# A recurrent mixer with fp32 gate and block products, and the last output panel of the split products summed in one half of its PSUM bank

## The chip, the cores and the metric

The kernel runs on one core of one Trainium2 chip. Its time is the device time of one execution in microseconds: 3352.14 us is the median of three runs (3350.11 to 3352.18). The engines are PE (TensorE, matmul), DVE (VectorE), ACT (ScalarE), POOL (GpSimd) and SP, which here issues the loads of the weights.

## The reference, cut to what matters

A residual stream x of 256 tokens and 1024 features goes through six layers. Each is a feed-forward sublayer, a mixer, and a second feed-forward sublayer, so there are 12 feed-forward sublayers (FFN) and 6 mixers: HGRN, differential attention, pooling, HGRN, a hybrid of a state-space model and attention (HYB), and the recurrent mixer (REC). Each sublayer normalizes its input and its output:

```python
h = swiglu_2(rms_norm(x, g[0]), ffn_w_in, ffn_w_out)      # silu(x @ gate) * (x @ up) @ w_out, d_ff = 2816
x = x + 0.5 * rms_norm(h, g[1])
h = recurrent_mixer(rms_norm(x, g[2]), ...)
x = x + rms_norm(h, g[3])

def recurrent_mixer(h, w_in, conv_w, conv_b, w_a, b_a, w_x, b_x, lam, w_out):
    gate, xr = jnp.split(h @ w_in, 2, axis=-1)            # 1024 -> 2 x 1024
    gate = jax.nn.gelu(gate, approximate=True)
    xr = causal_conv(xr, conv_w, conv_b)                  # 4 taps along the tokens
    return (rg_lru(xr, w_a, b_a, w_x, b_x, lam) * gate) @ w_out

def rg_lru(x, w_a, b_a, w_x, b_x, lam):                   # 8 blocks of 128 x 128 in w_a and in w_x
    r = sigmoid(block_product(x, w_a) + b_a)
    i = sigmoid(block_product(x, w_x) + b_x)
    log_a = 8 * r * log_sigmoid(lam)
    a = exp(log_a)
    u = sqrt(-expm1(2 * log_a)) * (i * x)
    return scan of s[t] = a[t] * s[t-1] + u[t]
```

## The kernel before

**Layout.** Everything lies by feature: h and the like are [128 partitions, 8 feature tiles, 256 tokens]. Weights come in panels of 1 MB (128 x 2048 fp32) that SP loads into 5 slots (raw); panel g is asked for when panel g - 5 is done.

**Split products.** Most products are made of fp32r parts. ACT copies a panel to whi (1.9 us), DVE makes wlo = raw - whi (2.3 us), which together is called a split. The input is split too: xs (or hs in the second half of an FFN) holds hi in columns 0:256 and lo in 256:512. `tile_product` (L1886, L1887) then does whi x [hi | lo], 512 columns, and wlo x hi, 256 columns, into a PSUM bank of 512 columns. The result is the sum of the bank's two halves. So ACT first copies the right half to corr (L1572) and DVE adds it to the left one (L1744), into tsum or y.

**Whole products.** The output projections of the mixers other than HYB read raw as plain fp32 with 256 moving columns (L2010). Each such product is two records in the trace, its result needs one half of the bank and no corr, and its panel no split. These panels are called whole.

**FFN.** 22 panels in, 11 out. Of the 11, seven ("wide") hold two rows of weights for all eight output tiles, and four hold the last eight rows for one pair of output tiles each. Both kinds add to the same banks. HYB's projection is built so with four wide panels.

**The close of a sublayer.** ACT squares the output tiles, PE sums the squares over the partitions (L1997, L2002, L2004, L2006, each two records), ACT makes the reciprocal root (L1504, L1506), DVE updates h (L1723, L1725) and splits it for the next sublayer, whose first two panels open with L1909 and L1911. The last two tiles, 6 and 7, are handled by themselves in `close_sublayer`: where the last panel is split, each goes corr (ACT, L1563), y (DVE, L1717), square (ACT, L1566); where it is whole, ACT squares the bank. Ten small matmuls (L1988) stand before the next sublayer's first product.

**REC.** PE does six split panels (four of x, two of the gate), the block products of W_a and W_x as split products in four quarters (L366, L367), two more gate panels, and the whole output projection. Between readouts DVE does the convolution with all its taps (L378, L385) pair by pair and splits its result for the block (L223). Then come sigmoids (ACT, L265), log a, i x conv, Exp and Tanh (ACT, L270, L275), one minus a squared (DVE, L333, L336), its root (ACT, L280), the products and scans (DVE, L345, L347), Gelu (ACT, L282) and the gated product (DVE, L351), which the projection waits for.

**What sets the order.** Each engine's instructions stand in the order in which its function (`act_rec`, `dve_rec`, `pe_rec`; `read_out` calls a hook after each panel) writes them, and it waits on named semaphores. Nothing reorders them.

Of the kernel before, what the change touches and what calls it, by code (L numbers as in the profile page):

```python
# [9 lines left out]
F32 = mybir.dt.float32  # L10
F32R = mybir.dt.float32r
# [47 lines left out]
def build(nc, a, out):  # L59
# [22 lines left out]
    for l in range(2):  # L82
# [13 lines left out]
    log1ps = hgrns = seconds = 0  # L96
    for n, s in enumerate(subs):
        s["n"], s["fill"] = n, fills
        fills += 1
        s["ls0"], s["it"], s["seconds"] = log1ps, hgrns, seconds  # L100
        seconds += s["kind"] == REC
        log1ps += s["kind"] in (HYB, REC)
        hgrns += s["kind"] == HGRN
        s["closes_with_y"] = sum(not t["segs"][-1].whole for t in subs[:n])
# [13 lines left out]
    with ctx:  # L118
# [48 lines left out]
        xs2 = nc.alloc_sbuf_tensor_at("xs2", [P, KD, 2 * T], F32R, offset=mix_offset + (MB - 2) * KD * T * 4)  # L167
# [47 lines left out]
        def hi_of_second(act, s, pair, src):  # L215
            q = slice(2 * pair, 2 * pair + 2)
            act.wait_ge(sem("second_ready"), 4 * s["seconds"] + SECOND_ORDER[s["kind"]].index(pair) + 1)
            nc.scalar.activation(xs2[:, q, 0:T], src[:, q, :], ACT.Copy).then_inc(sem("second_hi"), 1)

        def lo_of_second(dve, s, pair, src):  # L220
            q = slice(2 * pair, 2 * pair + 2)
            dve.wait_ge(sem("second_hi"), 4 * s["seconds"] + SECOND_ORDER[s["kind"]].index(pair) + 1)
            nc.vector.tensor_tensor(xs2[:, q, T:2 * T], src[:, q, :], xs2[:, q, 0:T].bitcast(F32), ALU.subtract  # L223
                                    ).then_inc(sem("second_lo"), 1)

        SECOND_ORDER = {REC: (0, 1, 2, 3)}


        R_GATE, R_X, R_CONV, R_CORR, R_R, R_I, R_A, R_TH = (mix[:, b] for b in range(8))


        def rec_dst(p):
            return R_X[:, 2 * p:2 * p + 2, :] if p < 4 else R_GATE[:, 2 * p - 8:2 * p - 6, :]


        REC_QUARTERS = ((0, 0, R_R), (1, 0, R_I), (0, 4, R_R), (1, 4, R_I))

        def act_rec(act, s, read_out, split, rstd):
            seg = s["segs"][1]

            def hook(p):
                if p == 1:
                    act.wait_ge(sem("log1p_negabs"), s["ls0"] + 1)
                    nc.scalar.activation(rec_col[:, 0, :], rec_col[:, 0, :], ACT.Exp).then_inc(sem("log1p_exp"), 1)
                elif p == 3:
                    act.wait_ge(sem("log1p_w"), s["ls0"] + 1)
                    nc.scalar.activation(rec_col[:, 3, :], rec_col[:, 1, :], ACT.Ln).then_inc(sem("log1p_ln"), 1)
                if 1 <= p <= 4:
# [1912 lines left out]
```

## Time and profile before

| | |
|---|---|
| median of three runs | 3352.14 us |
| profiled execution | 3345.8 us, span 3344.1 us |
| busy in it | PE 3141.9 us (94%), DVE 2293.2 (69%), ACT 1737.4 (52%) |
| chain that ended last | PE 79%, DVE 10%, ACT 6% |
| mean granted TensorE clock | 0.971 |
| REC sublayer | from 3018.3 to 3146.5 us |

Durations of single instructions are of the profiled execution. Matmuls overlap: the time that one costs is the distance from its start to the next one's start, and not its own duration. Rows of the chain give such pieces, rows of the timeline give an instruction's start and duration. "[0.84 <-ACT mix L1566]" at a row's end is idle time of the engine before it, and what ended it.

### The profile page before, as it was taken

What the parts mean: (1) busy time and instruction counts of PE and PEld (TensorE: products, weight loads), DVE (VectorE), ACT (ScalarE), POOL (GpSimd) and SP (SyncE); (2) the same over time, 40 slices, a digit from 0 to 9 for tenths busy, and PEclk for the clock granted to TensorE, in tenths of its full rate; (3) what the DMA queues carried; (4) which work ended last, traced back from release to release, by engine and by line L of the source; (5) the groups of instructions that cost most, each with busy time, mean ns of one, the idle gap of its engine ahead of it and who ended that gap; (6) DMA issues with size and microseconds to landing.
All of it is one profiled execution on the core that took longest, in us unless ns stands there. A gap on an engine that the chain in (4) does not pass through costs nothing.

```text
span 3344.1 us, 43867 instructions
## 1 busy us (share of the span) xinstructions
PE 3141.9 (94%) x17560; PEld 2704.5 (81%) x17560; DVE 2293.2 (69%) x2787; ACT 1737.4 (52%) x2100; POOL 4.3 (0%) x21
## 2 busy tenths in 40 slices
PE   9998999998899999999998899999787999997798
PEld 8876888887688888888886788888675888886687
DVE  7667575857486776676857576775865675857674
ACT  6455554645464653555545555555443554544553
POOL 0000000000000000000000000000000000000000
PEclk9998999999899999999999899999897999998899
DMA  6542354553255454454553245454330454553353
GB/s 231 189 151 101 132 191 168 192 190 134 90 177 191 174 189 163 162 190 171 191 180 126 81 173 190 175 189 175 140 126 1 170 191 168 192 192 120 115 188 125
DMA packets 75354, 534.73 MB, mean 160 GB/s; under 512 B 8480, under 2 KB 8608, under 8 KB 10784
## 3 DMA queue, kind: packets, MB, share of 16 engines
q1 hardware_dynamic: 75168, 532.07, 44.6%
q8 instruction: 139, 2.28, 0.3%
q14 instruction: 47, 0.39, 0.0%
HBM read 530.99 MB, written 1.05 MB: 159 GB/s over the span
## 4 chain that ended last, share of the span: by engine, by line
PE 79%; DVE 10%; ACT 6%; DVEq 3%; issue 1%; DMA 0%; SPq 0%; ACTq 0%
PE pp L1886 35%; PE pp L1887 18%; PE pm L1886 8%; PE pp L2010 4%; PE pm L1887 4%; PE pp L1909 4%; DVE wlo L1667 3%; PE pp L1911 2%; ACT whi L1500 2%; ACT corr L1572 1%; DVEq L382 1%; DVE mix L1829 1%; DVE mix L385 0%; DVE h L1725 0%; PE pp L1405 0%
## 5 line engine op out<-in xcount | busy, mean ns | idle before, releaser
L1886 PE MATMUL pp<-xs,whi 128*128 128x512 f32 x4912 | 1737.9, 399 | 27.6 <-DVE tsum L1744 25.8
L1667 DVE TENSOR_TENSOR wlo<-raw,whi 128x2048 fp32r<-128x2048 f32 x482 | 1101.8, 2289 | 425.2 <-ACT whi L1500 424.6
L1887 PE MATMUL pp<-xs,wlo 128*128 128x256 f32 x4912 | 1372.0, 279 | 0.0
L1886 PEld LDWEIGHTS pp<-xs,whi 128*128 128x128 f32 x4912 | 931.1, 190 | 256.3 <-issue 39.5
L1500 ACT ACTIVATE whi<-raw 128x2048 fp32r<-128x2048 f32 x482 | 918.9, 1910 | 283.5 <-DMA raw<-weights 282.6
L1887 PEld LDWEIGHTS pp<-xs,wlo 128*128 128x128 f32 x4912 | 933.1, 190 | 0.7 <-issue 0.2
L1572 ACT ACTIVATE corr<-pp 128x512 f32<-128x512 f32 x356 | 211.7, 595 | 564.0 <-PE pp L1887 538.4
L1744 DVE TENSOR_TENSOR tsum<-pp,corr 128x512 f32<-128x512 f32 x343 | 236.4, 689 | 295.1 <-ACT corr L1572 294.5
L1886 PE MATMUL pp<-hs,whi 128*128 128x512 f32 x1120 | 395.8, 394 | 0.0
L1886 PE MATMUL pm<-hs,whi 128*128 128x512 f32 x1120 | 393.0, 392 | 0.0
L1887 PE MATMUL pm<-hs,wlo 128*128 128x256 f32 x1120 | 313.1, 280 | 0.0
L1887 PE MATMUL pp<-hs,wlo 128*128 128x256 f32 x1120 | 313.1, 280 | 0.0
L1886 PEld LDWEIGHTS pm<-hs,whi 128*128 128x128 f32 x1120 | 210.2, 188 | 46.5
L1886 PEld LDWEIGHTS pp<-hs,whi 128*128 128x128 f32 x1120 | 210.3, 188 | 46.3
L1887 PEld LDWEIGHTS pp<-hs,wlo 128*128 128x128 f32 x1120 | 210.2, 188 | 0.3
L1887 PEld LDWEIGHTS pm<-hs,wlo 128*128 128x128 f32 x1120 | 210.3, 188 | 0.0
L1909 PE MATMUL pp<-xs,whi 128*128 128x512 f32 x576 | 166.2, 400 | 16.2 <-DVE xs L1678 16.2
L1584 ACT ACTIVATE hs<-hid 128x512 fp32r<-128x512 f32 x132 | 83.6, 633 | 109.7 <-DVE hid L1760 109.7
L2010 PE MATMUL pp<-mix,raw 128*128 128x256 f32 x512 | 115.6, 388 | 18.1 <-DVE mix L351 18.1
L2010 PEld LDWEIGHTS pp<-mix,raw 128*128 128x128 f32 x512 | 100.1, 196 | 35.0 <-issue 20.9
L1909 PEld LDWEIGHTS pp<-xs,whi 128*128 128x128 f32 x576 | 95.5, 188 | 33.5 <-issue 22.5
L1528 ACT ACTIVATE xs<-h,vec 128x256 fp32r<-128x256 f32 x119 | 60.5, 508 | 92.0 <-DVE h L1725 92.0
(335 smaller groups left out, 2390.9 us busy)
## 6 DMA issues: line engine op xcount, KB each, us to landing
raw<-weights SPq DMA_DIRECT2D x503, 1024.0 KB, 4.8
raw<-weights SPq DMA_DIRECT2D x8, 256.0 KB, 7.2
h<-x_by_feature SPq DMA_DIRECT2D x4, 256.0 KB, 6.2
out<-h SPq DMA_DIRECT2D x4, 256.0 KB, 2.5
vec<-vectors SPq DMA_DIRECT2D x1, 264.0 KB, 2.9
lamrow<-diff_lambda SPq DMA_DIRECT2D x1, 128.0 KB, 11.5
skiprow<-ssm_d SPq DMA_DIRECT2D x1, 8.0 KB, 12.3
```

Source lines behind the costliest of these rows:

```text
L382: dve.drain()
L1500: nc.scalar.activation(whi[:, slot, :], raw[:, slot, :], ACT.Copy).then_inc(sem("weights_hi"), 1)
L1528: nc.scalar.activation(xs[:, k, 0:T], h[:, k, :], ACT.Copy, scale=vec[:, k, s["gain"]:s["gain"] + 1]).then_inc(sem("x_hi"), 1)
L1572: nc.scalar.activation(two(corr[:, half, :]), banks[:, :, T:2 * T], ACT.Copy).then_inc(sem("corr_copied"), 1)
L1584: nc.scalar.activation(hs[:, 2 * j:2 * j + 2, 0:T], two(hid[:, :]), ACT.Copy).then_inc(sem("hidden_hi"), 1)
L1667: v.tensor_tensor(wlo[:, slot, :], raw[:, slot, :], whi[:, slot, :].bitcast(F32), ALU.subtract).then_inc(sem("weights_lo"), 1)
L1744: v.tensor_tensor(to, banks[:, :, 0:T], two(corr[:, half, :]), ALU.add).then_inc(sem("panel_out"), 1)
L1886: mm(bank, whi[:, slot, c:c + P], x_k, start=start, stop=False)
L1887: return mm(bank[:, 0:T], wlo[:, slot, c:c + P], x_k[:, 0:T], start=False, stop=stop)
L1909: e = mm(bank, whi[:, slot, c:c + P], xs[:, k, :], start=(k == 0), stop=(k == KD - 1))
L1911: e = mm(bank[:, 0:T], wlo[:, slot, c:c + P], xs[:, k, 0:T], start=False, stop=False)
L2010: return mm(in_banks[p % 2][:, ft, 0:T], raw[:, g % SLOTS, c:c + P], x[:, k, :], start=start, stop=stop)
```

## The change

There are two parts. Neither changes what is computed beyond rounding.

**The last output panel.** In the FFNs and HYB, the products for output tiles 6 and 7 use `summed_product`: whi x hi, whi x lo and wlo x hi, three matmuls of 256 columns, all into columns 0:256 of the bank. The bank then holds the sum, and `close_sublayer` takes squares and scaled output from it, as for whole panels.

**REC.** The four x panels stay split. The first gate panel, the block and the other three gate panels are whole: plain fp32 from raw, with R_IN = h x gain (eight ACT copies into y, `rec_in`) as the moving operand of the gate. The normalizing factor comes in when DVE reads the gate's bank (`gate_in`). The order on PE is now x, first gate panel, block in two halves, three gate panels, projection. ACT does the first tap of the convolution (`first_tap`), DVE the other three; sigmoids read PSUM; Exp, Tanh and the root go by halves, and Gelu and the gated product by pairs.

```diff
@@ -88,20 +88,19 @@
                 Segment("hyb_out", 8, wide=4)]))
         else:
             subs.append(dict(kind=REC, gain=g + 2, segs=[
-                Segment("rec_in_first", 6), Segment("rec_block", 1, reads=0), Segment("rec_in_last", 2), out_proj("rec_out")]))
+                Segment("rec_x", 4), Segment("rec_gate_first", 1, reads=0, whole=True), Segment("rec_block", 1, reads=0, whole=True),
+                Segment("rec_gate_last", 3, reads=0, whole=True), out_proj("rec_out")]))
         subs.append(ffn(9 + 2 * l, g + 4))
 
     panels = reads = fills = ffns = 0
...
@@ -212,96 +210,90 @@
...
+        R_IN = y
...
         def act_rec(act, s, read_out, split, rstd):
...
+            xseg = s["segs"][0]
+            def first_tap(p):
+                act.wait_ge(sem("rec_x"), p + 1)
+                for k in (2 * p, 2 * p + 1):
+                    e = nc.scalar.activation(R_CONV[:, k, :], R_X[:, k, :], ACT.Identity, bias=vec[:, k, VEC_REC_CONV_B:VEC_REC_CONV_B + 1],
+                                             scale=vec[:, k, VEC_REC_CONV_W + 3:VEC_REC_CONV_W + 4])
+                e.then_inc(sem("rec_tap"), 1)
             def hook(p):
...
+                if p == 0:
...
+                first_tap(p - 1)
+                if p == 1:
...
+                    for k in range(KD):
+                        e = nc.scalar.activation(R_IN[:, k, :], h[:, k, :], ACT.Copy, scale=vec[:, k, s["gain"]:s["gain"] + 1])
+                    e.then_inc(sem("rec_in"), 1)
+            read_out(xseg, s, after_first=lambda: rstd(rpre[:, :], 2 * s["n"]), hook=hook)
+            first_tap(3)
...
+            for t in range(2):
+                for buf, (dst, bias_row) in enumerate(((R_R, VEC_REC_BA), (R_I, VEC_REC_BX))):
+                    if (t, buf) == (1, 1):
+                        act.wait_ge(sem("panel_done"), s["segs"][2].g0 + 1)
+                    else:
+                        act.wait_ge(sem("rec_gates"), 2 * t + buf + 1)
+                    for k in range(4):
+                        c = 4 * t + k
+                        e = nc.scalar.activation(dst[:, c, :], rec_gates(buf, t)[:, k, :], ACT.Sigmoid,
+                                                 bias=vec[:, c, bias_row:bias_row + 1])
+                    e.then_inc(sem("rec_sigmoid"), 1)
...
+            for t, q in enumerate(halves):
+                act.wait_ge(sem("rec_log_a"), t + 1)
+                nc.scalar.activation(R_A[:, q, :], R_R[:, q, :], ACT.Exp).then_inc(sem("rec_a"), 1)
+                nc.scalar.activation(R_TH[:, q, :], R_R[:, q, :], ACT.Tanh).then_inc(sem("rec_tanh"), 1)
...
+            for t, q in enumerate(halves):
+                act.wait_ge(sem("rec_one_minus_a2"), t + 1)
+                nc.scalar.activation(R_TH[:, q, :], R_TH[:, q, :], ACT.Sqrt, scale=-1.0).then_inc(sem("rec_sqrt"), 1)
...
+            for p in range(4):
+                act.wait_ge(sem("rec_gate_out"), p + 1)
+                q = slice(2 * p, 2 * p + 2)
+                nc.scalar.activation(R_GATE[:, q, :], R_GATE[:, q, :], ACT.Gelu_apprx_tanh).then_inc(sem("rec_gelu"), 1)
...
+        def dve_rec(dve, s, read_out, split):
...
+            r2 = rpre[:, :].rearrange("p (a t) -> p a t", a=1).to_broadcast([P, 2, T])
+            def conv(p):
+                dve.wait_ge(sem("rec_tap"), p + 1)
+                for j in (2, 1, 0):
+                    d = 3 - j
+                    for k in (2 * p, 2 * p + 1):
+                        v.scalar_tensor_tensor(R_CONV[:, k, d:T], R_X[:, k, 0:T - d], vec[:, k, VEC_REC_CONV_W + j:VEC_REC_CONV_W + j + 1],
+                                               R_CONV[:, k, d:T], ALU.mult, ALU.add)
+                    dve.drain()
+                v.memset(small[:, 1:2], 0.0).then_inc(sem("rec_conv"), 1)
+            def hook(p):
                 if p == 0:
...
+                if p == 1:
...
+                if p >= 2:
+                    conv(p - 2)
+                if p == 2:
...
+            dve.drain()
...
+            read_out(s["segs"][0], s, lambda p: R_X[:, 2 * p:2 * p + 2, :], hook=hook)
+            conv(2)
+            conv(3)
+            def gate_in(p):
+                g = s["segs"][1].g0 if p == 0 else s["segs"][3].g0 + p - 1
+                dve.wait_ge(sem("panel_done"), g + 1)
+                v.tensor_tensor(R_GATE[:, 2 * p:2 * p + 2, :], in_banks[p % 2][:, :, 0:T], r2, ALU.mult).then_inc(sem("rec_gate_out"), 1)
+            gate_in(0)
+            for t, q in enumerate(halves):
+                dve.wait_ge(sem("rec_sigmoid"), 2 * t + 1)
+                for k in range(4 * t, 4 * t + 4):
+                    e = v.tensor_scalar(R_R[:, k, :], R_R[:, k, :], rec_col[:, 4, k:k + 1], None, ALU.mult)
+                e.then_inc(sem("rec_log_a"), 1)
+                dve.wait_ge(sem("rec_sigmoid"), 2 * t + 2)
+                v.tensor_tensor(R_I[:, q, :], R_I[:, q, :], R_CONV[:, q, :], ALU.mult)
+            gate_in(1)
+            for t, q in enumerate(halves):
+                dve.wait_ge(sem("rec_a"), t + 1)
+                v.tensor_tensor(R_A2[:, q, :], R_A[:, q, :], R_A[:, q, :], ALU.mult)
+                dve.drain()
+                dve.wait_ge(sem("rec_tanh"), t + 1)
+                v.scalar_tensor_tensor(R_TH[:, q, :], R_A2[:, q, :], 1.0, R_TH[:, q, :], ALU.add, ALU.mult
+                                       ).then_inc(sem("rec_one_minus_a2"), 1)
...
+            gate_in(2)
+            for t, q in enumerate(halves):
+                dve.wait_ge(sem("rec_sqrt"), t + 1)
                 v.tensor_tensor(R_I[:, q, :], R_I[:, q, :], R_TH[:, q, :], ALU.mult)
...
                 v.tensor_tensor_scan(flat2(R_R[:, q, :]), flat2(R_A[:, q, :]), flat2(R_I[:, q, :]), 0.0, ALU.mult, ALU.add)
...
+            gate_in(3)
+            for p in range(4):
+                dve.wait_ge(sem("rec_gelu"), p + 1)
+                q = slice(2 * p, 2 * p + 2)
                 v.tensor_tensor(R_A[:, q, :], R_R[:, q, :], R_GATE[:, q, :], ALU.mult).then_inc(sem("rec_gated"), 1)
...
+            def gate_panel(g, p):
+                slot = g % SLOTS
+                pe.wait_ge(sem(f"raw_landed_{slot}"), landings(g))
+                if p < 2:
+                    pe.wait_ge(sem("panel_out"), s["segs"][1].r0 + p - 1)
+                else:
+                    pe.wait_ge(sem("rec_gate_out"), p - 1)
+                for ft in range(2):
+                    for k in range(KD):
+                        c = k * PC + ft * P
+                        e = nc.tensor.matmul(in_banks[p % 2][:, ft, 0:T], raw[:, slot, c:c + P], R_IN[:, k, :], start=(k == 0),
+                                             stop=(k == KD - 1))
+                e.then_inc(sem("panel_done"), 1)
+            pe.wait_ge(sem("rec_in"), 1)
+            gate_panel(s["segs"][1].g0, 0)
+            block = s["segs"][2].g0
+            pe.wait_ge(sem(f"raw_landed_{block % SLOTS}"), landings(block))
+            for t in range(2):
+                for buf in range(2):
+                    if t:
+                        pe.wait_ge(sem("rec_sigmoid"), buf + 1)
+                    for k in range(4):
+                        if buf == 0 and k % 2 == 0:
+                            pe.wait_ge(sem("rec_conv"), 2 * t + k // 2 + 1)
+                        c = (buf * KD + 4 * t + k) * P
+                        e = nc.tensor.matmul(rec_gates(buf, t)[:, k, :], raw[:, block % SLOTS, c:c + P], R_CONV[:, 4 * t + k, :],
+                                             start=True, stop=True)
+                    e.then_inc(sem("panel_done" if t and buf else "rec_gates"), 1)
+            for p in range(1, 4):
+                gate_panel(s["segs"][3].g0 + p - 1, p)
+            pe.wait_ge(sem("rec_gate_out"), 4)
+            out_products(s, R_A, lambda k: pe.wait_ge(sem("rec_gated"), k // 2 + 1))
...
@@ -1557,12 +1570,7 @@
                         act.wait_ge(sem("last_tile_begun"), n + 1)
                     else:
                         act.wait_ge(sem("panel_done"), seg.g0 + seg.panels)
-                    if seg.whole:
-                        src = banks[:, t, 0:T]
-                    else:
-                        nc.scalar.activation(corr[:, 1, t * T:(t + 1) * T], banks[:, t, T:2 * T], ACT.Copy).then_inc(sem("last_corr"), 1)
-                        act.wait_ge(sem("last_out"), 2 * s["closes_with_y"] + t + 1)
-                        src = y[:, k, :]
+                    src = banks[:, t, 0:T]
                     nc.scalar.activation(sq[:, k, :], src, ACT.Square).then_inc(sem("last_squares"), 1)
                     e = nc.scalar.activation(upd[:, k, :], src, ACT.Copy, scale=vec[:, k, g:g + 1])
                 e.then_inc(sem("output_scaled"), 1)
@@ -1711,11 +1719,6 @@
                 n, seg = s["n"], s["segs"][-1]
                 output_squares(s, 1)
-                if not seg.whole:
-                    for t, k in enumerate((KD - 2, KD - 1)):
-                        dve.wait_ge(sem("last_corr"), 2 * s["closes_with_y"] + t + 1)
-                        v.tensor_tensor(y[:, k, :], in_banks[1][:, t, 0:T], corr[:, 1, t * T:(t + 1) * T], ALU.add
-                                        ).then_inc(sem("last_out"), 1)
                 dve.wait_ge(sem("rstd_ready"), 2 * n + 2)
...
+            def summed_product(bank, slot, c, x_k, start, stop):
+                mm(bank[:, 0:T], whi[:, slot, c:c + P], x_k[:, 0:T], start=start, stop=False)
+                mm(bank[:, 0:T], whi[:, slot, c:c + P], x_k[:, T:2 * T], start=False, stop=False)
+                return mm(bank[:, 0:T], wlo[:, slot, c:c + P], x_k[:, 0:T], start=False, stop=stop)
...
                         for k in range(2):
-                            e = tile_product(out_banks[ft // 2][:, ft % 2, :], (seg.g0 + p) % SLOTS, k * D + ft * P,
-                                             hs[:, wide_rows[2 * p + k], :], p + k == 0, False)
+                            product = summed_product if ft >= KD - 2 else tile_product
+                            e = product(out_banks[ft // 2][:, ft % 2, :], (seg.g0 + p) % SLOTS, k * D + ft * P,
+                                        hs[:, wide_rows[2 * p + k], :], p + k == 0, False)
                     e.then_inc(sem("panel_done"), 1)
...
                         for k in range(KD):
-                            e = tile_product(out_banks[pair][:, ft, :], g % SLOTS, k * PC + ft * P, hs[:, last_rows[k], :],
-                                             False, k == KD - 1)
+                            product = summed_product if pair == 3 else tile_product
+                            e = product(out_banks[pair][:, ft, :], g % SLOTS, k * PC + ft * P, hs[:, last_rows[k], :],
+                                        False, k == KD - 1)
                         if pair == 3 and ft == 0:
                             e.then_inc(sem("last_tile_begun"), 1)
```

What stands on ACT at the end of an FFN's close. Before, from the last readout on (corr 128x256 is one tile's right half, y the sum):

```order
L1572 ACTIVATE corr<-pp 128x512
L1541 ACTIVATE mix<-y 128x512
L1548 ACTIVATE mix<-y,vec 128x256 x2
L1563 ACTIVATE corr<-pp 128x256
L1566 ACTIVATE mix<-y 128x256
L1567 ACTIVATE mix<-y,vec 128x256
L1563 ACTIVATE corr<-pp 128x256
L1566 ACTIVATE mix<-y 128x256
L1567 ACTIVATE mix<-y,vec 128x256
L1504 ACTIVATE rln<-pm,eps 128x256
```

In the changed kernel, the same place on ACT:

```order
L1580 ACTIVATE corr<-pp 128x512
L1554 ACTIVATE mix<-y 128x512
L1561 ACTIVATE mix<-y,vec 128x256 x2
L1574 ACTIVATE mix<-pp 128x256
L1575 ACTIVATE mix<-pp,vec 128x256
L1574 ACTIVATE mix<-pp 128x256
L1575 ACTIVATE mix<-pp,vec 128x256
L1517 ACTIVATE rln<-pm,eps 128x256
```

The two corr copies are gone, and the squares read pp, which is PSUM.

What stands on PE between the two output tiles of an FFN's last panel. Before (L1997 is the first sum of squares):

```order
L1886 MATMUL pp<-hs,whi 128x512
L1887 MATMUL pp<-hs,wlo 128x256
L1997 MATMUL pm<-mix,ones 128x256
L1886 MATMUL pp<-hs,whi 128x512
L1887 MATMUL pp<-hs,wlo 128x256
```

In the changed kernel, there:

```order
L1891 MATMUL pp<-hs,whi 128x256
L1892 MATMUL pp<-hs,whi 128x256
L1893 MATMUL pp<-hs,wlo 128x256
L2010 MATMUL pm<-mix,ones 128x256
L1891 MATMUL pp<-hs,whi 128x256
L1892 MATMUL pp<-hs,whi 128x256
L1893 MATMUL pp<-hs,wlo 128x256
```

One matmul more stands in each product, with the same whi as its neighbour, and the sums keep their place.

What stands on PE in REC behind the last split panel ahead of the block, with the waits. Before (xs_51 is the split convolution):

```order
L1886 MATMUL pp<-xs,whi 128x512
L1887 MATMUL pp<-xs,wlo 128x256
L366 MATMUL pp<-xs_51,whi 128x512 [waits weights_lo,panel_out,second_lo]
L367 MATMUL pp<-xs_51,wlo 128x256
L366 MATMUL pp<-xs_51,whi 128x512
L367 MATMUL pp<-xs_51,wlo 128x256
```

In the changed kernel, behind the last x panel (y is R_IN, mix the convolution):

```order
L362 MATMUL pp<-y,raw 128x256 [waits panel_out,raw_landed_3,rec_in]
L362 MATMUL pp<-y,raw 128x256 x15
L378 MATMUL pm<-mix,raw 128x256 [waits rec_conv,raw_landed_4]
L378 MATMUL pm<-mix,raw 128x256
L378 MATMUL pm<-mix,raw 128x256 [waits rec_conv]
L378 MATMUL pm<-mix,raw 128x256 x5
L378 MATMUL pm<-mix,raw 128x256 [waits rec_conv,rec_sigmoid]
L378 MATMUL pm<-mix,raw 128x256
L378 MATMUL pm<-mix,raw 128x256 [waits rec_conv]
L378 MATMUL pm<-mix,raw 128x256
L378 MATMUL pm<-mix,raw 128x256 [waits rec_sigmoid]
L378 MATMUL pm<-mix,raw 128x256 x3
```

A gate panel stands ahead of the block, the block waits for the convolution in pairs of tiles, and its second half for the sigmoids that free its banks.

## Rows read from the trace of the kernel before

**Rows 1.** The page: part 1, part 4 by engine, and part 5, PE's costliest weight loads.
```profile
PE 3141.9 (94%) x17560; PEld 2704.5 (81%) x17560; DVE 2293.2 (69%) x2787; ACT 1737.4 (52%) x2100; POOL 4.3 (0%) x21
...
PE 79%; DVE 10%; ACT 6%; DVEq 3%; issue 1%; DMA 0%; SPq 0%; ACTq 0%
...
L1886 PEld LDWEIGHTS pp<-xs,whi 128*128 128x128 f32 x4912 | 931.1, 190 | 256.3 <-issue 39.5
```

**Rows 2.** Windows: REC's panels 3 and 4, its projection, HGRN's projection.
```profile
core 0: us, PE busy (x) PEld busy (x) DVE busy (x) ACT busy (x) POOL busy (x), PEclk, DMA share, GB/s
3029.97:3041.74 11.77, 11.77 (x66) 10.06 (x66) 10.37 (x17) 4.15 (x6) 0.00 (x0) 1.00 0.71 262
...
3111.81:3138.22 26.41, 26.41 (x113) 22.94 (x114) 6.86 (x6) 9.38 (x12) 0.00 (x0) 0.92 0.32 107
353.60:377.77 24.17, 24.17 (x113) 21.28 (x113) 7.54 (x8) 12.10 (x16) 0.00 (x0) 1.00 0.33 116
```

**Rows 3.** Waits in REC, 3018.28 to 3146.5: total us, times, longest.
```profile
PE pp L2010 <- DVE mix L351: 18.1, 1, 18.1
...
PE pp L1886 <- DVE tsum L1744: 10.5, 2, 5.9
...
PE pp L366 <- issue: 5.0, 1, 5.0
```

**Rows 4.** Timeline of PE at an FFN's close: start, duration, instruction.
```profile
3005.24 0.39 PE L1886 MATMUL pp<-hs,whi 128*128 128x512 f32 x1
...
3009.05 0.39 PE L1886 MATMUL pp<-hs,whi 128*128 128x512 f32 x1
...
3012.61 0.59 PE L2002 MATMUL pm<-mix,ones 128*128 128x256 f32 x2
...
3014.48 0.70 PE L2006 MATMUL pm<-mix,ones 128*128 128x256 f32 x2 [0.84 <-ACT mix L1566]
...
3018.28 0.47 PE L1909 MATMUL pp<-xs,whi 128*128 128x512 f32 x1 [0.95 <-DVE xs L1678]
```

**Rows 5.** Timeline of PE at REC's close, whose last panel is whole.
```profile
3141.94 0.59 PE L2002 MATMUL pm<-mix,ones 128*128 128x256 f32 x2
3142.37 0.59 PE L2004 MATMUL pm<-mix,ones 128*128 128x256 f32 x2
3142.80 0.59 PE L2006 MATMUL pm<-mix,ones 128*128 128x256 f32 x2
...
3146.51 0.70 PE L1909 MATMUL pp<-xs,whi 128*128 128x512 f32 x2 [0.96 <-DVE xs L1678]
```

**Rows 6.** The chain at the FFN's close: start, length of the piece, what.
```profile
3013.25 0.28 ACT corr L1563
3013.55 0.44 DVE y L1717
3014.01 0.42 ACT mix L1566
```

**Rows 7.** The chain: a run of eight 256-column fp32r matmuls, and fp32 records.
```profile
3019.44 0.95 PE pp L1911 x8
...
3138.65 3.45 PE pp L2010 x16
```

**Rows 8.** Timeline of DVE in REC.
```profile
3034.57 0.69 DVE L1829 TENSOR_TENSOR mix<-tsum,rpre 128x512 f32<-128x512 f32 x1 [0.73 <-ACT rpre L1506]
...
3038.37 2.78 DVE L385 SCALAR_TENSOR_TENSOR mix<-mix,vec 128x255 f32<-128x255 f32 x6
...
3096.62 1.23 DVE L333 TENSOR_TENSOR mix<-mix 128x1024 f32<-128x1024 f32 x1 [1.75 <-ACT mix L270]
...
3103.10 1.23 DVE L345 TENSOR_TENSOR mix<-mix 128x1024 f32<-128x1024 f32 x1
...
3110.43 2.36 DVE L351 TENSOR_TENSOR mix<-mix 128x1024 f32<-128x1024 f32 x2
```

**Rows 9.** Timeline of ACT in REC.
```profile
3084.57 6.51 ACT L265 ACTIVATE mix<-mix,vec 128x256 f32<-128x256 f32 x16
...
3099.18 1.06 ACT L280 ACTIVATE mix<-mix 128x1024 f32<-128x1024 f32 x1 [0.81 <-DVE mix L336]
```

More of the change, by code:

```diff
@@ L95, in build @@
     splits_before, whole_panels = [], set()
-    log1ps = hgrns = seconds = 0
+    log1ps = hgrns = 0
     for n, s in enumerate(subs):
@@ L99, in build @@
         fills += 1
-        s["ls0"], s["it"], s["seconds"] = log1ps, hgrns, seconds
-        seconds += s["kind"] == REC
+        s["ls0"], s["it"] = log1ps, hgrns
         log1ps += s["kind"] in (HYB, REC)
         hgrns += s["kind"] == HGRN
-        s["closes_with_y"] = sum(not t["segs"][-1].whole for t in subs[:n])
         if s["kind"] == FFN:
@@ L212, in tok @@
             return flat2(buf).rearrange("p (a d) -> p a d", a=TT)
[L215 to L236, printed above, removed]
-        def act_rec(act, s, read_out, split, rstd):
-            seg = s["segs"][1]
+        R_GATE, R_X, R_CONV, R_R, R_I, R_A, R_A2, R_TH = (mix[:, b] for b in range(8))
@@ L259, in act_rec @@
-            split(seg.g0 + AHEAD)
-            def sigmoids(slot):
-                dst, bias_row = ((R_R, VEC_REC_BA), (R_I, VEC_REC_BX))[slot]
-                act.wait_ge(sem("rec_read"), 3 + slot)
-                for k in range(KD):
-                    e = nc.scalar.activation(dst[:, k, :], dst[:, k, :], ACT.Sigmoid, bias=vec[:, k, bias_row:bias_row + 1])
-                e.then_inc(sem("rec_sigmoid"), 1)
-            def gates(p):
-                if p == 0:
-                    nc.scalar.activation(R_A, R_R, ACT.Exp).then_inc(sem("rec_a"), 1)
@@ L272, in act_rec @@
-            sigmoids(0)
-            sigmoids(1)
-            act.wait_ge(sem("rec_log_a"), 1)
-            nc.scalar.activation(R_TH, R_R, ACT.Tanh)
-            read_out(s["segs"][2], s, hook=gates)
-            for half in range(2):
-                act.wait_ge(sem("rec_one_minus_a2"), half + 1)
-                q = slice(4 * half, 4 * half + 4)
-                nc.scalar.activation(R_TH[:, q, :], R_TH[:, q, :], ACT.Sqrt, scale=-1.0).then_inc(sem("rec_sqrt"), 1)
-            act.wait_ge(sem("rec_gates"), 1)
@@ L311, in hook @@
                     dve.drain()
-            read_out(s["segs"][0], s, rec_dst, hook=hook)
-            for n, (slot, k0, dst) in enumerate(REC_QUARTERS):
-                dve.wait_ge(sem("rec_corr"), n + 1)
-                half = slice(4 * slot, 4 * slot + 4)
-                v.tensor_tensor(dst[:, k0:k0 + 4, :], (pp, pm)[slot][:, :, 0:T], R_CORR[:, half, :], ALU.add
-                                ).then_inc(sem("rec_read"), 1)
-            split(seg.g0 + AHEAD)
-            dve.wait_ge(sem("rec_sigmoid"), 1)
@@ L342, in dve_rec @@
+            gate_in(1)
[6 more added lines that the diff above has]
+                                       ).then_inc(sem("rec_one_minus_a2"), 1)
             v.memset(R_A[:, :, 0:1], 0.0)
-            for half, q in enumerate(halves):
-                dve.wait_ge(sem("rec_sqrt"), half + 1)
+            gate_in(2)
@@ L1826, in read_out @@
                         signal = {"k": "at_keys_in", "v": "at_values_in"}.get(kind)
+                    elif s["kind"] == REC:
+                        signal = "rec_x"
                     if kind == "v" and group:
```

86 lines of the change are left out of this document (17 added, 69 removed).

## The prediction

> **What bounds the kernel now.** I read the page's shares first, then the chain of waits, then the REC sublayer by windows and waits, and last the closes of two sublayers beside each other. PE is busy 94% of the span, and 79% of the chain that ended last is PE; a weight load takes 190 ns but lies beside the matmuls [rows 1]. So whatever PE does more or less of moves the end directly, and what ACT and DVE save counts only where PE waits for them. Such places are few. In REC PE waits 18.1 us for DVE's last product before the output projection, 10.5 us for readouts, and 5.0 us before the block products [rows 3]; here it is DVE's serial chain (convolution, gates, scan) that ends last, not PE. The other place is the close of every sublayer: from the first column-sum matmul after the last product (L2002) to the next sublayer's first product it takes 18.28 - 12.61 = 5.67 us where the last panel is split [rows 4], and 46.51 - 41.94 = 4.57 us where it is "whole" [rows 5]. In the first, PE waits 0.84 us for ACT's square (L1566), because the last tile goes ACT corr, DVE y, ACT square, and each step is a piece of the chain [rows 6]; in the second the eight sum records run without a gap.
>
> **Part 1, the closes.** 13 sublayers (12 FFN and HYB) close with a split panel. The change lets the last two output tiles sum in PSUM, so ACT squares them there; corr and y go. What is left is the whole close's shape. Is PE then the bound? The four records of L2002 and L2004 need 0.86 us (41.94 to 42.80 in rows 5); ACT's one square of 0.4 us behind the last product fits under that, as it does in the whole close. DVE's fold for L2002 is ready, since L2002 to L2004 has no gap now. So each close gains 5.67 - 4.57 = 1.10 us, 13 x 1.10 = 14.3 us. (The very last has no sublayer behind it, and may give some tenths less.)
>
> The price: tiles 6 and 7 take three matmuls of 256 columns instead of one of 512 and one of 256. Per FFN these are 7 wide panels x 2 tiles x 2 rows plus 16 products of the last panel, 44; HYB has 4 x 2 x 2 + 16 = 32; in all 12 x 44 + 32 = 560 products, each with one matmul and one weight load more. A product now takes 3.81 us / 11 = 0.346 us (3005.24 to 3009.05, [rows 4]). Eight matmuls of 256 columns, each with weights of its own, take 0.95 us, 0.119 each [rows 7], so three take 0.357: +0.0105 x 560 = +5.9 us, all on PE's path. The lower bound is the same number of streamed columns at no extra cost, 0 us. The upper bound is a weight load of 190 ns that nothing hides [rows 1]: 3 x 0.19 = 0.57 us a product, +125 us; I take the row of eight, the same kind of instruction at the same width, and +5.9. Three writes in a row to the same 256 columns of PSUM are new at 0.119 spacing; the fp32 products write their 256 columns again every 0.216 us without a gap [rows 7], which is wider and so only half an answer.
>
> The Trainium skill ("TensorE: Matmul & The Clock Gate", sections "LDWEIGHTS" and "Back-to-back issue gap") gives a load as columns / 1.2, 107 ns, and a warm gap of N/2.4 + 2.5 ns. As an estimate by that page three matmuls take 0.3275 us against 0.325 for the pair, +1.4 us in all instead of +5.9, with the load just under the matmul that should hide it. The trace disagrees in size: its 256-column spacing is 119 ns where the page has 109 [rows 7].
>
> **Part 2, REC.** The stage is rebuilt: only four x panels are split, the gate panels and the block go to PE as plain fp32 from raw, and the gate panels stand behind the block. I follow it on the clock of the trace before; the opening pair and x panels 3 and 4 stay as they are, so PE is free at 3041.7 [rows 2].
> - *First gate panel.* 16 products of two records; an x16 run of records takes 3.45 us, so a product takes 0.431 and a panel 6.9 us [rows 7]. It waits for rec_in: ACT's rpre ends just before DVE's L1829 at 3034.57 [rows 8]; then come the Exp, two first taps, Ln, and eight copies at 0.41 (16 in 6.51, [rows 9]), about 3039.8, and then a copy of corr (0.6) and DVE's add (0.7) by 3041.0. PE does not wait: 3041.7 to 3048.7.
> - *Convolution.* DVE no longer does the first tap nor the splits of later panels between readouts. Six taps take 2.78 us, 2.9 with the drain [rows 8]. x panel 3 is read by 3041.8, then: conv 0 by 3044.7, small columns and panel 4's readout by 3046.8, conv 1 by 3049.7, conv 2 by 3052.6, conv 3 by 3055.5.
> - *Block.* Tiles 0 and 1 follow the gate panel at once, tiles 2 and 3 wait for conv 1 (3049.7), all W_a and W_x of half 0 end at 3052.4; half 1 waits for conv 2 and conv 3 (3055.5) and ends at 3058.1. PE waits about 3.5 us in all here; ACT's sigmoids (4 in 1.6 us) are ready before their bank is needed.
> - *Gate panels 2 to 4.* 3 x 6.9: they end at 3065.0, 3071.9 and 3078.8. Meanwhile DVE has log a and I x conv done by 3061.4 and stands before gate_in(1) until 3065.1; that wait is new, and queued behind it are the squares and the one-minus. They take 4.9 (four of 1.22, [rows 8]), to 3070.8. ACT's Exp and Tanh halves (1.06 each, [rows 9]) with their table loads end at 3065.6, in time. DVE then stands at gate_in(2) until 3071.9.
> - *The tail.* gate_in(2) 0.75; two products and two scans 7.33 us (3103.10 to 3110.43, [rows 8]) give 3080.1; gate_in(3) 0.7, then Gelu of the fourth pair on ACT beside DVE's first gated product 0.7: PE starts the output projection at 3081.6, having waited 2.8 us. Before, it started at 3111.8: 30.2 us sooner.
> - *The projection itself.* Its first 112 records took 26.41 us at a granted clock of 0.92; in HGRN, with PE busy ahead of it, 24.17 at 1.00 [rows 2]. PE comes from 20 us of nearly dense matmul instead of 18 us of waiting, so I take the 2.2 us too.
> REC gives 30.2 + 2.2 = 32.4 us, although its 80 products that become fp32 cost 80 x (0.431 - 0.346) = 6.8 us more PE time; that is inside the steps above. The freed ACT and DVE time in REC (five splits each) is worth nothing beyond this. The weight loads do not bind: each of the stage's later panels is asked for five panels ahead, at least 20 us before its use.
>
> **Sum.** -14.3 + 5.9 - 32.4 = -40.8 us. The profiled execution took 3345.8 us (span 3344.1), so 3305.0 like for like; it lies 6.3 us under the median of the timed runs, 3352.14, and against that the forecast is **3311.3 us**.
>
> **Rivals.**
> - *The clock falls inside REC.* The new stage has PE waits near 3049, 3055 and 3079, and the convolutions leave PE half busy. One cold start costs 2.2 us (26.41 against 24.17); with the projection cold and one or two more in the block and the gate panels, 4 to 7 us of REC go: about 3316.5. For it: the stage before shows 0.92 at its end [rows 2]; against: the waits are 0.5 to 2.8 us, not 18.
> - *The close gives nothing.* If the sums then wait for something else (DVE's fold behind its 2.3 us split, or ACT's scale of tile 6 before the last square), only the third matmul's price stays: 3352.1 - 32.4 + 5.9 = 3325.6. Against: in the whole closes of this trace the same chain runs without a gap [rows 5].
> - *The change is slower.* The third weight load is not hidden: with two 256-column matmuls ahead instead of a 512 the array waits for weights. It is decided at 46.7 / 560 = 0.083 us more per product, because the other parts give 46.7. At the full 190 ns a load it is +0.224 x 560 = +125 us, 3352.1 - 46.7 + 125 = 3431. Against it stands the run of eight at 0.119 [rows 7]; for it only that the trace has no run longer than eight.
> - *The rebuilt REC does not start sooner*, since a step that I have hidden (rec_in, the fp32 panels) is late: the chain of DVE is the shorter part, and it would have to grow by 30 us. I leave it to the tail.
>
> **Chances.** The forecast 0.70, its own range 3305 to 3318; the falling clock 0.15 (3313 to 3320); no gain in the close 0.08 (3325.6); slower through weight loads 0.03; other losses 0.04. The range 3303 to 3322 holds the first two with the spread of the runs. A difference under about 0.2%, 6.7 us, cannot be told from none; faster by more holds in all but the last two cases: 0.95; same 0.02; slower 0.03.
>
> **What would show it.** Right: L2006's successor of an FFN close with no wait for ACT, 4.6 us from the first sum record to the next first product; a triple in 0.357 us; in REC the 18.1 us wait gone, PE waits of 3 to 4 us in the block, 2 to 3 before the projection, and the projection's first 112 records in 24.2. Wrong: a triple over 0.37 us (each 0.01 is 5.6 us), a close still over 5 us, or PE waiting for rec_in or between gate panels.

## The result, and the profile after

| | before | changed |
|---|---|---|
| median of the timed runs | 3351.12 us (3348.41 to 3352.18, 4 runs) | 3307.97 us (3307.34 to 3310.86, 4 runs) |
| profiled execution | 3345.8 us, span 3344.1 | 3310.86 us, span 3309.1 |

The ratio is 0.9874, 95% interval 0.9857 to 0.9891; the forecast was 3311.3 us, range 3303 to 3322. The two medians are 43.2 us apart, the two profiled executions only 35; where those 8 us are is told below.

The page of the changed kernel, for [rows 1]. PE's share rises since PE has the work and the waits are gone:

```profile
PE 3148.8 (95%) x18120; PEld 2741.2 (83%) x18120; DVE 2259.5 (68%) x2738; ACT 1716.2 (52%) x2078; POOL 4.2 (0%) x21
...
PE 83%; DVE 8%; ACT 5%; DVEq 3%; issue 1%; DMA 0%; SPq 0%; ACTq 0%
```

PE has 560 matmuls more, as counted. The timeline of PE at the close of the feed-forward sublayer before REC (start, duration, instruction), for [rows 4, 6]:

```profile
3007.20 0.28 PE L1891 MATMUL pp<-hs,whi 128*128 128x256 f32 x1
3007.32 0.28 PE L1892 MATMUL pp<-hs,whi 128*128 128x256 f32 x1
3007.43 0.28 PE L1893 MATMUL pp<-hs,wlo 128*128 128x256 f32 x1
...
3009.31 0.28 PE L1891 MATMUL pp<-hs,whi 128*128 128x256 f32 x1
...
3009.66 0.60 PE L2015 MATMUL pm<-mix,ones 128*128 128x256 f32 x2
3010.09 0.59 PE L2017 MATMUL pm<-mix,ones 128*128 128x256 f32 x2
3010.53 0.59 PE L2019 MATMUL pm<-mix,ones 128*128 128x256 f32 x2
...
3014.23 0.47 PE L1920 MATMUL pp<-xs,whi 128*128 128x512 f32 x1 [0.95 <-DVE xs L1686]
```

The wait for ACT's last square is gone, and from the first sum record to the next first product it is 14.23 - 9.66 = 4.57 us, the whole close's figure [rows 5], down from 5.67. Six triples take 3009.31 - 3007.20 = 2.11 us, 0.352 each.

PE in REC. The stage starts at 3014.23 here, and at 3018.28 before; so 4.05 has to be added to compare with the prediction's clock:

```profile
3037.53 7.07 PE L362 MATMUL pp<-y,raw 128*128 128x256 f32 x32
3044.44 3.98 PE L378 MATMUL pm<-mix,raw 128*128 128x256 f32 x16
...
3048.68 1.10 PE L378 MATMUL pm<-mix,raw 128*128 128x256 f32 x4 [0.27 <-DVE small L286]
3051.49 2.86 PE L378 MATMUL pm<-mix,raw 128*128 128x256 f32 x12 [1.71 <-DVE small L286]
3054.19 20.88 PE L362 MATMUL pp<-y,raw 128*128 128x256 f32 x96
3077.57 26.10 PE L2023 MATMUL pp<-mix,raw 128*128 128x256 f32 x112 [2.49 <-DVE mix L346]
```

The first gate panel starts at 3041.58 on that clock (forecast 3041.7), the last wait for the convolution ends at 3055.54 (3055.5), the block at 3058.24 (3058.1), and the projection starts at 3081.62 (3081.6). Behind it, though, the window from its first record to the one behind the first 112, and the piece of it up to 3080.99, for [rows 2] (us, busy of PE, PEld, DVE, ACT, POOL, granted clock, DMA share, GB/s):

```profile
3077.57:3103.50 25.93, 25.93 (x113) 22.58 (x113) 7.37 (x8) 10.60 (x13) 0.00 (x0) 0.93 0.35 130
3077.57:3080.99 3.42, 3.42 (x8) 2.79 (x9) 1.66 (x3) 1.22 (x1) 0.00 (x0) 0.50 0.47 189
```

It takes 25.9 us at a clock of 0.93, not 24.2 at 1.00. Up to 3080.99 the granted clock is 0.50 (1.2 GHz): this start is cold too. DVE's tail ahead of it, for [rows 8]:

```profile
3068.20 0.69 DVE L316 TENSOR_TENSOR mix<-pp,rpre 128x512 f32<-128x512 f32 x1 [1.31 <-PE pp L362]
3068.81 1.22 DVE L338 TENSOR_TENSOR mix<-mix 128x1024 f32<-128x1024 f32 x1
...
3076.13 0.69 DVE L316 TENSOR_TENSOR mix<-pp,rpre 128x512 f32<-128x512 f32 x1
3076.74 2.49 DVE L346 TENSOR_TENSOR mix<-mix 128x512 f32<-128x512 f32 x4
```

DVE stands 1.31 us before the third gate panel, with the scans queued behind it, and PE stands for DVE afterwards.

The expectations below name 25.7 us for these records and a wait of 2.9 us ahead of them. The 25.7 are a window that ends where the last of them starts, and the 2.9 are the wait of PE's weight loads; PE's matmuls waited 2.5.

**Stretches.** A program of this kind has a clean measure in its own trace: the time from one sublayer's first product (L1909, after: L1920) to the next one's. All in us, each from one profiled execution:

| kernel | feed-forward | HGRN, attention, pooling, HGRN, HYB | REC |
|---|---|---|---|
| before | 190.27 | 184.8, 155.5, 68.8, 190.6, 314.4 | 128.23 |
| before, again | 190.27 | 184.9, 156.3, 68.9, 190.6, 317.5 | 128.45 |
| changed | 189.47 | 184.6, 156.9, 67.2, 193.7, 317.3 | 97.73 |
| changed, again | 189.47 | 186.2, 157.1, 67.2, 189.1, 314.8 | 97.55 |
| the close alone | 189.47 | 184.6, 157.1, 67.3, 189.2, 318.5 | 127.75 |
| REC alone | 190.28 | 184.9, 156.4, 68.9, 190.6, 317.3 | 97.74 |
| close reads half | 189.17 | 184.6, 155.6, 67.2, 192.0, 320.2 | 128.13 |
| halved pairs | 190.77 | 184.9, 157.2, 67.2, 190.6, 316.6 | 127.81 |

The feed-forward value is that of the ten or so that repeat within 0.1 us (the first and last sublayer differ). These stretches repeat, and REC's within 0.7 us among the kernels that leave it as it was, within 0.2 among those that change it alike. Pooling repeats too, at two values: 68.8 to 68.9 in both profiles of the kernel before and in that of REC alone, 67.2 to 67.3 in all others of the table. The rest move by up to 5.8 us. PE's clock moves with them. These are the windows of pooling and HYB before, of pooling in the changed kernel, and of HYB where the close reads half:

```profile
1302.67:1371.51 68.84, 63.95 (x308) 54.60 (x309) 39.88 (x75) 26.95 (x44) 0.00 (x0) 0.98 0.40 138
2323.30:2637.74 314.44, 265.55 (x1392) 217.67 (x1393) 207.86 (x371) 128.49 (x185) 0.00 (x0) 0.90 0.30 104
...
1299.04:1366.28 67.24, 62.37 (x308) 53.37 (x309) 39.88 (x75) 26.95 (x44) 0.00 (x0) 1.00 0.39 141
...
2313.37:2633.60 320.23, 272.31 (x1392) 222.37 (x1393) 206.98 (x369) 127.70 (x183) 0.00 (x0) 0.87 0.28 102
```

In pooling DVE's and ACT's busy time is the same in both, and PE's is 1.58 us more at a clock of 0.98 than at 1.00. HYB is longest of the table where its clock is 0.87, and takes 5.8 us less at 0.90. What shifts the clock in a part that nobody touched stays open.

### The profile page after: what moved, and what is told of

Its sections match the earlier page's. It is cut to its first block, busy times and chain, and to the rows that moved or that the text cites. A ratio compares the mean times of both kernels' runs of the same rounds, so it can differ in the third digit from the quotient of the medians.

```text
span 3309.1 us, 44902 instructions
## 1 busy us (share of the span) xinstructions
PE 3148.8 (95%) x18120; PEld 2741.2 (83%) x18120; DVE 2259.5 (68%) x2738; ACT 1716.2 (52%) x2078; POOL 4.2 (0%) x21
## 4 chain that ended last, share of the span: by engine, by line
PE 83%; DVE 8%; ACT 5%; DVEq 3%; issue 1%; DMA 0%; SPq 0%; ACTq 0%
PE pp L1897 33%; PE pp L1898 17%; PE pm L1897 8%; PE pp L2023 4%; PE pm L1898 4%; PE pp L1920 4%; DVE wlo L1675 2%; PE pp L1892 2%; PE pp L1891 2%; PE pp L1893 2%; PE pp L1922 2%; ACT whi L1513 1%; DVE mix L1834 1%; ACT corr L1580 1%; DVEq L395 0%
## 5 line engine op out<-in xcount | busy, mean ns | idle before, releaser
L1897 PE MATMUL pp<-xs,whi 128*128 128x512 f32 x4848 | 1713.1, 398 | 16.7 <-DVE tsum L1747 15.0
L1675 DVE TENSOR_TENSOR wlo<-raw,whi 128x2048 fp32r<-128x2048 f32 x477 | 1090.6, 2289 | 423.8 <-ACT whi L1513 423.2
L1898 PE MATMUL pp<-xs,wlo 128*128 128x256 f32 x4848 | 1356.1, 280 | 0.0
L1897 PEld LDWEIGHTS pp<-xs,whi 128*128 128x128 f32 x4848 | 917.7, 189 | 238.9 <-issue 28.9
L1513 ACT ACTIVATE whi<-raw 128x2048 fp32r<-128x2048 f32 x477 | 909.5, 1910 | 283.4 <-DMA raw<-weights 282.8
L1898 PEld LDWEIGHTS pp<-xs,wlo 128*128 128x128 f32 x4848 | 921.0, 190 | 0.7 <-issue 0.2
L1897 PE MATMUL pp<-hs,whi 128*128 128x512 f32 x560 | 198.6, 392 | 0.0
L1920 PE MATMUL pp<-xs,whi 128*128 128x512 f32 x576 | 166.2, 400 | 16.4 <-DVE xs L1686 16.4
L1891 PE MATMUL pp<-hs,whi 128*128 128x256 f32 x560 | 159.2, 284 | 0.0
L1892 PE MATMUL pp<-hs,whi 128*128 128x256 f32 x560 | 156.9, 280 | 0.0
L1897 PEld LDWEIGHTS pp<-hs,whi 128*128 128x128 f32 x560 | 105.1, 188 | 23.2
L1920 PEld LDWEIGHTS pp<-xs,whi 128*128 128x128 f32 x576 | 95.5, 188 | 33.9 <-issue 22.8
```

The source lines that it names most:

```text
L1513: nc.scalar.activation(whi[:, slot, :], raw[:, slot, :], ACT.Copy).then_inc(sem("weights_hi"), 1)
L1675: v.tensor_tensor(wlo[:, slot, :], raw[:, slot, :], whi[:, slot, :].bitcast(F32), ALU.subtract).then_inc(sem("weights_lo"), 1)
L1891: mm(bank[:, 0:T], whi[:, slot, c:c + P], x_k[:, 0:T], start=start, stop=False)
L1892: mm(bank[:, 0:T], whi[:, slot, c:c + P], x_k[:, T:2 * T], start=False, stop=False)
L1897: mm(bank, whi[:, slot, c:c + P], x_k, start=start, stop=False)
L1898: return mm(bank[:, 0:T], wlo[:, slot, c:c + P], x_k[:, 0:T], start=False, stop=stop)
```

## The experiments

My theory was the sum: a shorter close, 1.10 us 13 times; a price of some ns for each third matmul; and REC's projection 30 us sooner. The rivals were a close worth nothing, and a third weight load that is not hidden.

**The close alone.** To the kernel before, only the first part:

```diff
+                            product = summed_product if ft >= KD - 2 else tile_product
...
+                    src = banks[:, t, 0:T]
```

> The kernel before with the first part of the change alone: three matmuls of 256 columns for output tiles 6 and 7, and the close reads their bank; REC stays as before. Theory (the close saves 1.10 us 13 times, the third matmul costs 5 to 7 ns in each of 560 products, 3 to 4 us): 14.3 - 3.5 = 10.8 us less, ratio 0.9968. My sum's price of 10.5 ns: 8.4 us less, 0.9975. Rival (the close gives nothing): 3 to 6 us more, ratio 1.001 to 1.002.

Measured: 3337.16 us (8 runs), ratio 0.9969, interval 0.9958 to 0.998. The feed-forward stretch falls by 0.80 us. A close that gives nothing is excluded.

**REC alone.** The changed kernel with the old close.

```diff
+                        act.wait_ge(sem("last_out"), 2 * s["closes_with_y"] + t + 1)
+                        src = y[:, k, :]
```

> The changed kernel with the close as before (corr, y and the pair of matmuls for tiles 6 and 7), so REC's rebuild alone. Theory: 30.5 us less as in REC's stretch of the profile, up to 32.4, ratio 0.9903 to 0.9909. Rival (the two parts overlap, or REC's gain is given back in the next sublayer): under 27 us less, ratio over 0.992.

Measured: 3319.85 us, ratio 0.9914 (0.99 to 0.9927). REC's stretch is 97.74 us, 30.5 less, the feed-forward stretch as before. The two parts' ratios multiply to 0.9883, within the changed kernel's interval: the two parts add up within the noise.

**The close reads half.** The gain of the close without its price:

```diff
-                    if seg.whole:
-                        src = banks[:, t, 0:T]
-                    else:
...
+                    src = banks[:, t, 0:T]
```

> The kernel before, with the close reading the left half of the bank of tiles 6 and 7 while the products stay a pair of matmuls; the output of these tiles lacks the whi x lo term. It has the gain of the shorter close without the third matmul. Theory: 13 x 1.10 = 14.3 us less, ratio 0.9957, and the difference to the kernel with the third matmul is that matmul's price, 3 to 4 us. Rival (the close is worth less, and the matmul is free): equal to it, both 0.997.

Measured: 3335.03 us, ratio 0.9957 (0.9944 to 0.9971). The stretch is 189.17, exactly 1.10 us under before. So the 44 triples cost 189.47 - 189.17 = 0.30 us, 7 ns each.

**Halved pairs.**

```diff
+                mm(bank[:, 0:T], whi[:, slot, c:c + P], x_k[:, 0:T], start=start, stop=False)
+                mm(bank[:, T:2 * T], whi[:, slot, c:c + P], x_k[:, T:2 * T], start=start, stop=stop)
```

> The kernel before, where in every wide panel but the first the 512-column matmul of all eight output tiles is done as two of 256 into the two halves of the bank: 12 x 96 + 48 = 1200 products with one matmul and one weight load more, and no other change. It measures the price of the third matmul alone, without three writes in a row to the same columns. Theory (5.5 to 7 ns each): 6.6 to 8.4 us more, ratio 1.0020 to 1.0025. My sum's 10.5 ns: 12.6 us more, 1.0038. Rival (the price comes from the same columns written three times in a row, and a third matmul alone costs nothing): 0, ratio 1.000. Rival (a load is not hidden, 190 ns): over 200 us more.

Measured: 3356.29 us (10 runs), ratio 1.0024 (1.0014 to 1.0033). The stretch grows by 0.50 us for 96 products, 5.2 ns each. The load of 190 ns is hidden in long runs too, which its row alone did not show:

```profile
159.82 0.28 PE L1886 MATMUL pp<-hs,whi 128*128 128x256 f32 x1
...
161.58 0.28 PE L1886 MATMUL pm<-hs,whi 128*128 128x256 f32 x1
```

That is 1.76 us for five products, 0.352. Most of the third matmul's price needs no repeated columns; where the remaining 1.6 ns of the seven come from stays open.

**The third gate panel is read between the scans.** Of the changed kernel one line is moved:

```diff
-            gate_in(2)
             for t, q in enumerate(halves):
...
+                if t == 0:
+                    gate_in(2)
```

> The changed kernel with one line moved: DVE reads the third gate panel (gate_in(2)) between the two scans and not ahead of both, so it does not stand waiting for that panel before it scans. Theory (DVE's tail from gate_in(2) on sets when the projection starts): it starts 1.3 us sooner, PE's wait before it is 1.5 instead of 2.9 us, and if the shorter wait also keeps the clock up, another 1.6 us: 1.3 to 2.9 us less than the changed kernel, ratio to the kernel before about 0.9865 where that is 0.9872. Rival (something else, the gate panels on PE, sets the start): no change in the stretch of REC.

Measured: 3304.86 us, ratio to the kernel before 0.9867 (0.985 to 0.9883). REC's stretch is 95.05 us, 2.7 less: the projection starts 1.0 us sooner, and its first 112 records are back at full clock. PE and the window:

```profile
3075.70 24.41 PE L2024 MATMUL pp<-mix,raw 128*128 128x256 f32 x112 [1.47 <-DVE mix L347]
```
```profile
3075.70:3099.95 24.25, 24.25 (x113) 21.36 (x114) 7.37 (x8) 10.59 (x13) 0.00 (x0) 1.00 0.43 154
```

By its stretch it beats both kernels; the timed medians, 3 us apart from the changed kernel's, are too close to say so.

**Matmuls of ones in the wait.**

```diff
+            keep_clock(5)
             pe.wait_ge(sem("rec_gate_out"), 4)
```

> The changed kernel with five small matmuls of ones (ten records, 2.2 us) in PE's wait before the output projection; their result is read by nobody. Theory (the projection starts at the low clock because PE stood still 2.9 us, and pays 1.6 us for it: 25.7 instead of 24.2 us for its first 112 records): 1.5 us less in REC's stretch, the start of the projection not moved. Rival (the slow start has another cause, such as waits within the projection for the gated tiles): its first 112 records still take 25.7 us.

Measured: 3305.99 us, ratio 0.9872 (0.9855 to 0.9888), and REC 96.06 us, 1.67 less than the changed kernel. The projection starts at the same place, 63.35 us into the stage, and runs warm:

```profile
3073.84 24.41 PE L2024 MATMUL pp<-mix,raw 128*128 128x256 f32 x112 [0.34 <-DVE mix L346]
```

**The block first.** The first gate panel goes behind the block:

```diff
-                Segment("rec_x", 4), Segment("rec_gate_first", 1, reads=0, whole=True), Segment("rec_block", 1, reads=0, whole=True),
+                Segment("rec_x", 4), Segment("rec_block", 1, reads=0, whole=True), Segment("rec_gate_first", 1, reads=0, whole=True),
...
```

> The changed kernel with the first gate panel behind the block, next to the other three, so that nothing covers the convolution on PE. Theory (the 6.9 us gate panel ahead of the block is what hides DVE's convolution): PE waits at the block for conv 1 and on, the block still ends at conv 3 plus 2.6 us, and then four gate panels stand instead of three: 6.9 us more than the changed kernel, plus up to 3 for a cold clock. Rival (the gate panel's place does not matter, since the tail on DVE sets the projection's start): 0 to 2 us more.

Measured: 3311.49 us, ratio 0.9886 (0.9869 to 0.9902). The projection starts 70.27 us into REC, not 63.34: 6.9 later, one gate panel. PE's waits in the stage, its records in the block and at the projection, and a window of the block:

```profile
PE pm L377 <- DVE small L286: 6.9, 3, 3.8
...
3042.46 5.76 PE L377 MATMUL pm<-mix,raw 128*128 128x256 f32 x16 [3.82 <-DVE small L286]
3048.39 2.86 PE L377 MATMUL pm<-mix,raw 128*128 128x256 f32 x12 [0.17 <-DVE small L286]
...
3081.37 24.41 PE L2023 MATMUL pp<-mix,raw 128*128 128x256 f32 x112 [2.50 <-DVE mix L346]
...
3042.46:3048.20 5.74, 5.74 (x16) 4.42 (x16) 5.28 (x13) 2.37 (x7) 0.00 (x0) 0.64 0.00 0
```

The stretch is 102.98 us, only 5.3 more, since here the projection started at full clock, though PE had waited the same 2.5 us ahead of it. So the wait's length alone does not say whether the clock falls. It did fall in the block, at the wait of 3.82 us (0.64 on average in the window), but DVE's last pair of the convolution came later still: its records start 37.3 us into REC in both kernels, so that cold stretch cost nothing.

**The first tap on DVE.**

```diff
+                dve.drain()
+                for k in (2 * p, 2 * p + 1):
+                    v.tensor_scalar(R_CONV[:, k, :], R_X[:, k, :], vec[:, k, VEC_REC_CONV_W + 3:VEC_REC_CONV_W + 4],
+                                    vec[:, k, VEC_REC_CONV_B:VEC_REC_CONV_B + 1], ALU.mult, ALU.add)
+                dve.drain()
```

> The changed kernel with the convolution's first tap back on DVE (two operations of 0.4 us and a drain in each of four pairs) and not on ACT. Theory: each conv step grows by 0.8 us, conv 3 ends 3.2 us later, and with PE waiting for it the block, the gate panels and the projection move by 3.2 us, all on the path; up to 1.6 more if a longer wait drops the clock. Rival (gate panels or tail bound the stage): under 1 us.

Measured: 3312.83 us, ratio 0.9892 (0.9875 to 0.9908); the projection starts 6.0 us later, which is more than I expected. The convolution ends 3.7 us later (3.2 expected; the edit has two drains a pair, and the expectation counts one); the rest is the clock. The last 12 records of the block, and their window:

```profile
3054.30 5.23 PE L378 MATMUL pm<-mix,raw 128*128 128x256 f32 x12 [2.66 <-DVE small L286]
```
```profile
3054.30:3059.36 5.06, 5.06 (x12) 4.06 (x13) 3.90 (x10) 1.57 (x4) 0.00 (x0) 0.52 0.00 0
```

They take 5.06 us at a clock of 0.52 (1.2 GHz) instead of 2.70 at full clock, after a wait of 2.66 us instead of 1.71.

**Short lo parts in REC before.**

```diff
+                if rec + 4 <= g < rec + 9:
+                    v.tensor_scalar(wlo[:, slot, :], raw[:, slot, :], 0.0, None, ALU.mult).then_inc(sem("weights_lo"), 1)
+                    return
```

> The kernel before, where DVE's subtraction for the lo part of REC's five panels after the fourth is one multiplication by zero with a single input (these panels' lo parts are zero, so the output lacks their share). By the nearest row, DVE's tensor_scalar of 256 columns at 0.275 us, it should take 1.1 to 1.2 us instead of 2.25. All five stand on DVE ahead of the block. Theory (DVE's queue, splits among it, is what PE waited for in REC before): the block starts 5 x 1.1 = 5.5 us sooner, and the stretch from REC's start to its projection is 87.9 instead of 93.5 us. Rival (ACT's hi copies, or the weights' landing, set the pace): under 2 us.

Measured: 3343.99 us (10 runs), ratio 0.9981 (0.9971 to 0.9991). The operation took 1.22 us:

```profile
3035.54 1.22 DVE L1669 TENSOR_SCALAR wlo<-raw 128x2048 fp32r<-128x2048 f32 x1
...
3106.40 26.00 PE L2014 MATMUL pp<-mix,raw 128*128 128x256 f32 x112 [17.98 <-DVE mix L351]
```

REC starts at 3018.61 here, so the projection starts 87.8 us into it, not 93.5. So DVE's queue set the pace of the stage before, and if every us off it comes back, as these 5.7 did, an estimate for all five subtractions is 5 x 2.25 = 11 us, about a third of the 30. The first tap on ACT and the place of the first gate panel have prices of their own in the two runs above, taken from the changed kernel; whether these add up with the 11 was not tried, and the work by halves and pairs has no run.

**Both kernels again.**

> The changed kernel once more, for a second profile. Theory (the mixers that the change does not touch take a varying time from one execution to the next): the twelve feed-forward sublayers and REC repeat within 0.3 us each, 97.7 for REC, while HGRN, attention, pooling and HYB together move by some us from the 919.7 of the first profile. Rival (the change costs them time, 5.5 us against before): again 919 to 920.

> The kernel before once more, for a second profile. Theory: the feed-forward sublayers 190.27 us again and REC 128.2, the other mixers anywhere from 914 to 920 us. Rival (the change costs the mixers time): again 914.

Measured: 3306.0 and 3349.74 us, 43.7 apart. The five other mixers take 914.2 and 918.1 us in the kernel before, 919.7 and 914.5 in the changed one. The single run of HGRN at 193.7 did not come back (189.1), though the kernel whose close reads half has 192.0.

## Why the prediction was right

**The bound.** PE's path and the few places where it waits were the right frame: every part changed the end by what it did to that path, and DVE's freed time counted where PE waited for DVE; the short lo parts showed it for REC, and nothing was tried elsewhere.

**The close, -14.3.** Right to the hundredth: 1.10 us per close, read from the whole close beside it. In HYB too, from the first sum record to the next first product, it went from 5.67 us (2632.08 to 2637.75) to 4.56 (2630.72 to 2635.28). The last sublayer gave less (its stretch fell by 0.48 us, price included), as noted.

**The third matmul, +5.9.** The mechanism was right, the size too high. A product's price was 7 ns, not 10.5: 560 x 7 = 3.9 us. The run of eight at 0.119 stood at the very start of a sublayer; in long runs a 256-column matmul takes 0.117. Why it was slower there stays open. The 190 ns of a load never showed. The 109 ns per matmul by the formula of the Trainium skill ("TensorE: Matmul & The Clock Gate", section "Back-to-back issue gap") were not reached either: the trace has 117.

**REC, -32.4.** The chain to the projection's start held within 0.15 us at four marks, 30.2 us in all. One reading on the way was off: the prediction has PE wait about 3.5 us in the block, but its own times leave 3058.1 - 3048.7 - 6.9 = 2.5, and measured it was 3054.19 - 3044.44 - 6.9 = 2.85, 2.0 of it in the two waits shown.

The step that failed is the 2.2 us for a warm projection: I had argued that PE comes from dense matmul, and it came from a wait of 2.5 us (my own chain had 2.8), with a cold start after it in both profiles of the changed kernel, in that of REC alone and in that of the first tap on DVE. It gave 0.3 us: from the first record to the one behind the first 112 it is 26.24 us before (3111.81 to 3138.05) and 25.93 after. The stretch gave 30.2 + 0.3 = 30.5. The keep-clock and moved-line kernels take 24.25 there and show the missing 1.7 us. The full term is 26.24 - 24.25 = 2.0, not 2.2, since the 26.41 of [rows 2] also hold the last record's own duration and the 24.17 do not.

**The sum.** -14.3 + 3.9 - 30.5 = -40.9 against the forecast -40.8: two sizes were off by 2 us with opposite signs, so that the sum came out within 0.1 is luck. The medians say -43.2, and the interval of the ratio is 36.5 to 47.9. The 2 us left over are no term of the change that I can show. Pooling's 1.6 us are of that size, and all eight profiles with the new close have them; but so has that of the halved pairs, which keeps the old close, and other mixers moved the other way. The profiles' -35 is explained by the other mixers, which took 5.5 us more in this profile than in that of before; in the second pair of profiles it was 3.6 us less; the median of the runs was the right thing to forecast against.

**The rivals.** The clock did fall at the projection and cost 1.7 us, a part of the first rival, which had it at 0.15; the block and the gate panels ran at full clock. The dead close and the exposed load are excluded by the runs of those parts.

## What to carry to other kernels

Two stages of one program that end alike, one with and one without an operation, price that operation better than its duration does. Where an engine's in-order queue decides, look at what stands first in it waiting for something late while ready work is behind it; here one moved line gave 2.7 us of REC's stretch. In a program whose parts run one after another, compare parts, not totals: the feed-forward stretch told 0.3 us where the timed runs of one kernel spread by 4 and more.

## What the runs showed that I had not expected

PE's clock fell to half (1.2 GHz) at a wait of 2.66 us in the kernel with the first tap on DVE and of 2.5 us in the changed kernel, but not at the same 2.5 us in the kernel with the block first, nor at one of 1.5. The mixers other than REC moved by up to 5.8 us from one profile to the next (HYB 314.4 to 320.2 us, at a mean clock of 0.90 and 0.87), while the feed-forward sublayers repeated to 0.1.
